# Two chained model blocks on one core: the norm in front of the expert queries made behind the projection ahead of it, search rounds of the key selection placed elsewhere, and filler products left out at three stages

## The chip, the cores and the metric

The kernel runs on one core of one Trainium2 chip. The metric is the device time of one launch in microseconds (us), as the median of several runs. Everything is float32, batch 1, 512 tokens, model width 1024.

## The reference, cut to what matters

The reference chains two model blocks. The first one mixes the tokens (a state space branch and a forgetting attention, merged, then projected by `w_out` and added to x) and then applies a product-key expert layer. The second has two layers, of which the even one has a sparse attention with an index search and a differential attention. The parts that the change touches:

```python
def rms_norm(x, g):                 # both blocks: x * rsqrt(mean(x*x) + eps) * g

def peer_ffn(h, w_query, sub_keys, u_tab, v_tab):       # h = rms_norm(x, ffn_norm_g)
    q = (h @ w_query).reshape(bsz, seq, 8, 2, 128)
    scores = jnp.einsum('blhcd,hckd->blhck', q, sub_keys)     # 16 x 128 scores a token
    s_top, i_top = lax.top_k(scores, 16)
    ...

def dsa_mixer(...):                 # sparse attention: scores of an indexer, best 128 keys of each query
    rel = jax.nn.relu(einsum('bqhd,bsd->bqhs', iq, ik) * IDX_DIM ** -0.5)
    score = jnp.einsum('bqhs,bqh->bqs', rel, iw)
    score = jnp.where(causal, score, -jnp.inf)
    _, idx = lax.top_k(score, k_sel)
    ...

def diff_mixer(...):                # two softmaxes a head, the second subtracted
    p = safe_softmax(s, causal)
    a = p[:, :, 0] - lam_full * p[:, :, 1]
    ...
```

## The kernel before, in words

**Stages.** The program is a row of stages. Each is a block with one instruction stream for each engine, and no engine enters the next stage before all have left the one before. x is kept transposed, as `xT`: 8 tiles of 128 channels by 512 tokens.

**Float32 products.** A float32 product is made as three products of halves (L137, L138, L139): the high half of each operand is made by ScalarE (`high_half`, L121), the low half by VectorE or GpSimd (`low_half`, L126). A tile of a projection is 128 output channels by 512 tokens, 8 tiles deep: 24 products. `projection` runs turns of `per_turn` tiles. SyncE loads the weights of a tile, ScalarE makes their high half as soon as the tile four earlier is through TensorE, GpSimd the low half, TensorE multiplies, and functions given as `evacuate` read the result; `before`, `after`, `between` and `behind_tile` add work of a stage at named places. `spin` (L132) issues products of a mask that nobody reads.

**The end of the first mixing.** `merge` (L2384) ends with the `w_out` projection (`project_add`): 8 tiles `ps` are added to `xT` by VectorE (L848) behind each tile.

**Expert queries (`peer_scores`, L2639).** The stage starts with `Norm`: ScalarE squares the 8 tiles of `xT` (L245), TensorE sums them with a matrix of ones (L250), then runs 30 spins, ScalarE takes the root (L257), VectorE inverts it (L269), then writes each normalised tile into `room` (L278); ScalarE and VectorE make its halves `h_high` and `h_low`, tile by tile. TensorE turns the sub keys in the wait (16 transposes, L2664, which need the keys' DMA, L2656) and then runs 16 query tiles in 4 turns of 4. ScalarE copies each query tile (L2691), TensorE multiplies it by its keys (L2679), ScalarE copies the scores (L2686), and VectorE searches the 16 best of them: MAX8 and its index, MATCH_REPLACE8, MAX8 and index again, each for 4 token tiles (L2767, L2770, L2774). Turns 1 to 3 are a hardware loop on VectorE, whose waits are made with register arithmetic (L71). A pair of copies (L2704) closes a turn. Behind the last tile TensorE makes products for the expert stage (`early_scores`).

**The even layer of block two.** `index_scores` makes the indexer's scores. The 128 best keys of a query are found in 16 rounds of `take_best` (MAX8, L3795, then MATCH_REPLACE8, L3798), for token tile [1] alone and for tiles [2, 3] together; tile 0 needs none. The rounds of tile [1] stand in `index_scores`, one behind each index head's step at t = 2 and at t = 3. Round 0 of [2, 3] stands in front of the differential attention's query tiles (`lead`), rounds 1 to 6 beside the query tiles, 7 and 8 inside the differential attention (`paired_attention`, L1483, by `beside` at its steps s = 1 and 2), 9 to 14 in front of `tile_norm`'s VectorE part in the following projection (`nope`), 15 behind it.

**Paired attention (L1483).** It is used three times (differential attention, sparse attention, odd layer). Each call starts with `spin(c, 0, 8)` on TensorE; then each step makes two sets of scores (L1551), VectorE takes the maxima (L1670), ScalarE the exponentials (L1614), GpSimd and VectorE scale and subtract them (L1633, L1663), TensorE transposes them and multiplies by the values (L1581).

The projection that ends the even layer's attention already does what `Feed` and `Late` say: in `project_add` with `next_gain` ScalarE makes the high half of gain * x (L321) and the squares (L323) behind each tile, VectorE the low half (L335) and the running sum (L339); the next stage sums that over channels (L363, L366), and its root follows late, beside products.

## Time and profile before

| | |
|---|---|
| median of 3 runs | 3316.16 us (3311.45 to 3322.05) |
| profiled execution | 3321.01 us, its span 3319.2 us |
| mean granted TensorE clock | 0.983 |
| TensorE busy | 97% of the span |
| VectorE, ScalarE, GpSimd busy | 54%, 41%, 39% |
| differential attention's stage | from about 2015 us to about 2065 us of the span |
| merge's last product to the first work of the stage behind the queries | 525.75 us to 667.67 us |

Each row of a timeline is start, duration, engine, line, operation, output and inputs, and how many instructions it groups; in brackets stands how long the engine was idle ahead of it and what released it. 97% is a mean over the whole span: at a stage's border or at a wait the engine stands still, and those places have to be read from the timeline.

### The profile page before, as it was taken

The numbers are of one execution on the slowest core, as the hardware profiler recorded it, in microseconds if no ns is written. First come the engines' busy times: TensorE is split into PE (matmuls) and PEld (weight loads), VectorE is DVE, ScalarE is ACT, GpSimd is POOL, SyncE is SP. The second block draws the span as 40 slices with busy tenths as digits, with TensorE's granted clock in tenths as the row PEclk, the third lists the DMA queues.
The fourth block names the chain that finished last, engine by engine and source line by source line (L and its number), as shares of the span: only waits on it lengthen the run. The fifth ranks groups of instructions, "written<-read, shape, count | busy, mean of one in ns | idle before, by whom it ended". The sixth has DMA issues, their size and how long they took to land. (4 is left out here: it accounts for less than half of the span.)

```text
span 3319.2 us, 47973 instructions
## 1 busy us (share of the span) xinstructions
PE 3208.2 (97%) x16487; PEld 2656.5 (80%) x16492; DVE 1779.2 (54%) x3737; ACT 1353.8 (41%) x2338; POOL 1286.2 (39%) x788
## 2 busy tenths in 40 slices
PE   7999999989999999999999998999999999999999
PEld 6877787889988888888888865578887874578887
DVE  6515324888958777777877467542211226632211
ACT  5234433247763333333333455332222436632322
POOL 2223352368852222222221323444444337644443
PEclk9999999999999999999999999999999989999999
DMA  5321242146679999999997421033333520033322
GB/s 126 84 73 33 76 114 78 57 138 212 224 286 344 321 325 321 328 317 330 318 323 263 118 54 36 13 95 95 95 91 93 130 64 1 18 91 95 100 85 82
DMA packets 453450, 501.83 MB, mean 151 GB/s; under 512 B 77360, under 2 KB 397808, under 8 KB 435392
## 3 DMA queue, kind: packets, MB, share of 16 engines
q1 hardware_dynamic: 429792, 363.05, 35.7%
q0 software_dynamic: 18432, 134.23, 11.0%
q10 hardware_dynamic: 5088, 2.75, 0.3%
q8 instruction: 82, 1.34, 0.2%
q14 instruction: 56, 0.46, 0.0%
HBM read 457.86 MB, written 38.80 MB: 150 GB/s over the span
## 5 line engine op out<-in xcount | busy, mean ns | idle before, releaser
L126 POOL TENSOR_TENSOR w_low<-w_ring,w_high 128x1024 fp32r<-128x1024 f32 (+2 forms) x316 | 745.2, 2362 | 1102.1 <-ACT w_high L121 1073.1
L137 PE MATMUL ps<-h_low,w_high 128*128 128x512 f32 (+1 forms) x2432 | 904.4, 372 | 27.3 <-PEq L640 15.4
L139 PE MATMUL ps<-h_high,w_low 128*128 128x512 f32 (+1 forms) x2432 | 896.7, 369 | 0.0
L138 PE MATMUL ps<-h_high,w_high 128*128 128x512 f32 (+1 forms) x2432 | 895.9, 368 | 0.0
L137 PEld LDWEIGHTS ps<-h_low,w_high 128*128 128x128 f32 x2432 | 460.1, 189 | 93.3 <-POOLq L629 14.1
L138 PEld LDWEIGHTS ps<-h_high,w_high 128*128 128x128 f32 x2432 | 460.4, 189 | 58.8 <-issue 1.0
L139 PEld LDWEIGHTS ps<-h_high,w_low 128*128 128x128 f32 x2432 | 459.6, 189 | 56.4
L121 ACT ACTIVATE w_high<-w_ring 128x1024 fp32r<-128x1024 f32 (+3 forms) x318 | 323.7, 1023 | 138.3 <-PE ps L139 121.2
L139 PE MATMUL ps<-v_high,top_at 128*128 128x512 f32 x768 | 300.3, 391 | 0.0
L138 PE MATMUL ps<-v_high,top 128*128 128x512 f32 x768 | 300.2, 391 | 0.0
L137 PE MATMUL ps<-v_low,top 128*128 128x512 f32 x768 | 299.0, 389 | 0.0
L121 ACT ACTIVATE v_high<-w_ring 128x1024 fp32r<-128x1024 f32 x128 | 135.5, 1059 | 261.4 <-PE ps L139 261.4
L2536 POOL DMA_INDIRECT room<-in_peer_uv_dram,idx_now x62 | 89.8, 1448 | 340.5 <-DVE sums L3391 340.5
L1633 POOL TENSOR_SCALAR probs<-probs,stat 128x128 f32<-128x128 f32 (+3 forms) x153 | 158.7, 1050 | 94.8 <-DVE stat L1644 57.1
L139 PEld LDWEIGHTS ps<-v_high,top_at 128*128 128x128 f32 x768 | 144.1, 188 | 30.2
L848 DVE TENSOR_TENSOR xT<-xT,ps 128x512 f32<-128x512 f32 (+1 forms) x40 | 27.5, 687 | 262.0 <-PE ps L139 262.0
L137 PEld LDWEIGHTS ps<-v_low,top 128*128 128x128 f32 x768 | 144.2, 188 | 28.5 <-issue 0.3
L138 PEld LDWEIGHTS ps<-v_high,top 128*128 128x128 f32 x768 | 144.1, 188 | 28.5
L126 DVE TENSOR_TENSOR v_low<-w_ring,v_high 128x1024 fp32r<-128x1024 f32 x128 | 156.1, 1219 | 0.0
L2536 POOL DMA_INDIRECT ring<-in_peer_uv_dram,idx_now x63 | 81.2, 1288 | 161.1 <-DVE sums L3391 132.4
L137 PE MATMUL ps<-a_low,w_high 128*128 128x512 f32 x352 | 136.9, 389 | 0.0
L138 PE MATMUL ps<-a_high,w_high 128*128 128x512 f32 x352 | 136.9, 389 | 0.0
(551 smaller groups left out, 5398.8 us busy)
## 6 DMA issues: line engine op xcount, KB each, us to landing
w_ring<-in_peer_uv_dram SPq DMA_DIRECT2D x128, 512.0 KB, 5.7
u_raw<-in_peer_uT_dram SPq DMA_DIRECT2D x78, 512.0 KB, 5.7
w_ring<-in_peer_uT_dram SPq DMA_DIRECT2D x50, 512.0 KB, 3.8
w_ring<-in_ffn_w_gate_dram SPq DMA_DIRECT2D x44, 512.0 KB, 3.7
w_ring<-in_ffn_w_up_dram SPq DMA_DIRECT2D x44, 512.0 KB, 3.8
w_ring<-in_w_in_dram SPq DMA_DIRECT2D x36, 512.0 KB, 3.8
w_ring<-in_ffn_w_down_dram SPq DMA_DIRECT2D x32, 448.0 KB, 3.7
peer_gates<-room SPq DMA_DIRECT2D x6, 2048.0 KB, 8.0
```

Source lines behind the costliest of these rows:

```text
L121: return nc.scalar.activation(rounded(high), whole, ACT.Copy)
L126: return eng.tensor_tensor(rounded(low), whole, high, ALU.subtract)
L137: nc.tensor.matmul(out, rounded(w_high), rounded(x_low), start=start, stop=False, **more)
L138: nc.tensor.matmul(out, rounded(w_high), rounded(x_high), start=False, stop=False, **more)
L139: return nc.tensor.matmul(out, rounded(w_low), rounded(x_high), start=False, stop=stop, **more)
L848: nc.vector.tensor_tensor(d, d, c.ps[:, first_bank + b + (tiles * (i % 2) if alternate else 0), :], ALU.add).then_inc(bank_free, w.parts)
L1633: nc.gpsimd.tensor_scalar(of, of, inverse[:, s % p_bufs, a:a + 1], None, ALU.mult).then_inc(normed_pool, 1)
L2536: self.c.nc.gpsimd.indirect_dma_start(self.ring[slot], None, self.uv, bass.IndirectOffsetOnAxis(ap=index, axis=0)).then_inc(self.gathered[ ...
```

## The change

1. **Norm in front of the expert queries.** `merge` is given the gain of the expert layer's norm and passes it to `project_add`, which so feeds the next stage as the even layer's does: L321, L323, L335, L339 run behind each of the 8 `w_out` tiles, and 16 spins end the stage on TensorE. `peer_scores` uses `Late` for the sum and the root. The first turn's 4 query tiles are made from gain * x without the norm's factor, and their scores are scaled for each token while ScalarE copies them (4 copies of 128x128 instead of one of 128x512). VectorE writes the normalised x into `room`; the new class `Renewed` rewrites `h_high` during the first turn's last tile (ScalarE, tile by tile, each behind the product that reads the old one), the odd low halves on VectorE, ahead of its second search, the even ones on GpSimd between two weight tiles. The key transposes stand behind the first query tile. VectorE's search is written out instead of looped.
2. **Search rounds.** Of tiles [2, 3], rounds 1 to 7 now stand beside the query tiles, none in the attention, 8 to 14 in front of `tile_norm`'s VectorE part, 15 behind it as before. Of tile [1], the 8 rounds of t = 2 stay, the other 8 stand at the end of the differential attention's VectorE program (`behind`).
3. **Spins.** The `spin(c, 0, 8)` at the start of the three paired attentions is left out.

```diff
@@ class Renewed (new)
+    def normalise(self, dve):
+        c = self.c
+        for k in range(KD):
+            c.nc.vector.scalar_tensor_tensor(self.whole[:, k, :], c.xT[:, k, :], c.gains[:, k:k + 1], c.rstd[:, :], ALU.mult, ALU.mult).then_inc(self.normed, 1)
+
+    def high_halves(self, act, wait_last):
+        for k in range(KD):
+            act.wait_ge(self.normed, k + 1)
+            if k < KD - 1:
+                act.wait_ge(self.used, k + 1)
+            else:
+                wait_last()
+            high_half(self.c.nc, self.c.h.high[:, k, :], self.whole[:, k, :]).then_inc(self.high, 1)
+
+    def low_halves(self, waiting, eng, odd):
+        c = self.c
+        for k in range(odd, KD, 2):
+            waiting.wait_ge(self.high, k + 1)
+            low_half(eng, c.h.low[:, k, :], self.whole[:, k, :], c.h.high[:, k, :]).then_inc(self.low[odd], 1)
+
+    def wait(self, pe, k):
+        pe.wait_ge(self.low[k % 2], k // 2 + 1)
@@ projection, gpsimd
         body(0, w.split)
-        turn_loop(pool, body, 1)
+        if renewed is not None:
+            body(1, 0, 2)
+            renewed.low_halves(pool, nc.gpsimd, 0)
+            body(1, 2)
+        turn_loop(pool, body, 1 if renewed is None else 2)
@@ projection, tensor
+                    if renewed is not None and b == 0 and not (isinstance(i, int) and i == 0):
+                        renewed.wait(pe, k)
...
+                    if renewed is not None and isinstance(i, int) and (i, b) == (0, per_turn - 1) and k < w.kt[b] - 1:
+                        mm.then_inc(renewed.used, 1)
@@ project_add
-            how["tail"] = (6, 16)
+            how["tail"] = (6 if alternate or first is None else 0, 16)
@@ paired_attention
-                spin(c, 0, 8)
...
+                if behind is not None:
+                    behind(dve)
@@ merge
-        project_add(c, w_out, c.xT, mixed_halves, ahead=ahead, first=first, ctx=ctx, ready=ready, first_bank=4)
+        project_add(c, w_out, c.xT, mixed_halves, ahead=ahead, next_gain=next_gain, first=first, ctx=ctx, ready=ready, first_bank=4)
@@ peer_scores
+        late, renewed = Late(c, ctx, rows=True), Renewed(c, ctx, room)
...
         def turn_keys(pe):
             pe.wait_ge(keys_in, 16)
+            pe.wait_ge(late.rooted, late.n)
...
-                nc.scalar.activation(scores[:, b, :, :], c.ps[:, 4 + b, :], ACT.Copy).then_inc(scores_out, 1)
+                if isinstance(i, int) and i == 0:
+                    for t in range(TT):
+                        last = nc.scalar.activation(scores[:, b, t, :], c.ps[:, 4 + b, t * P:(t + 1) * P], ACT.Copy, scale=c.rstd_rows[:, t:t + 1])
+                    last.then_inc(scores_out, 1)
+                else:
+                    nc.scalar.activation(scores[:, b, :, :], c.ps[:, 4 + b, :], ACT.Copy).then_inc(scores_out, 1)
 
             for b in range(per_turn):
+                if isinstance(i, int) and i == 0 and b == per_turn - 1:
+                    renewed.high_halves(act, lambda: wait_tile(b))
...
             for b in range(per_turn):
+                if i == 0 and b == 1:
+                    renewed.low_halves(dve, nc.vector, 1)
...
+        def prepare(dve):
+            late.invert(dve)
+            late.wait(dve)
+            renewed.normalise(dve)
...
-        project(c, w_query, {"act": copy, "pe": score, "dve": search}, ahead=ahead, after={"pe": early_scores}, before={"sp": load_keys, "pe": turn_keys, "act": move_keys}, norm=Norm(c, ctx, gain, c.h, squares=room))
+        project(c, w_query, {"act": copy, "pe": score, "dve": search}, ahead=ahead, after={"pe": early_scores},
+                before={"sp": load_keys, "pe": late.sum, "act_first": late.root, "act": move_keys, "dve": prepare},
+                between={1: {}}, behind_tile={(0, 0): turn_keys}, unrolled=("dve",), renewed=renewed)
@@ even layer
-                subln["dve"] = lambda dve: (search(dve, 0, 6), given(dve), search(dve, 6, None))
+                subln["dve"] = lambda dve: (search(dve, 0, 7), given(dve), search(dve, 7, None))
-    beside_tiles = 2 * DIFF_H - 2
+    beside_tiles = 2 * DIFF_H - 1
-    rest = [(n, tiles) for n in range(beside_tiles + 1, beside_tiles + 3)]
-
-    def beside(dve, s):
-        if 1 <= s <= len(rest):
-            take_best(c, Chain(dve, c.dve_step), score, best, left, rest[s - 1][1], rest[s - 1][0])
+
+    def behind(dve):
+        for n in range(DSA_H, rounds):
+            take_best(c, Chain(dve, c.dve_step), score, best, left, [1], n)
-    paired_attention(c, [head(s) for s in range(DIFF_H)], beside=beside, spare=oT[:, 0:2, :])
-    late = range(beside_tiles + 3, rounds)
+    paired_attention(c, [head(s) for s in range(DIFF_H)], spare=oT[:, 0:2, :], behind=behind)
+    late = range(beside_tiles + 1, rounds)
@@ index_scores
-            if t >= 2:
+            if t == 2:
                 take_best(c, step, score, best, left, [1], n - IH)
```

(The views of `weighed` in the expert stage are given names of their own at the same addresses.)

**TensorE from `merge` into the query stage.** Before, from merge's last product to the first query product (branch rows are the stage's border):

```order
L139 MATMUL ps<-mixed_high,w_low 128x512
L515 UNCONDITIONAL_BRANCH
L498 UNCONDITIONAL_BRANCH
L250 MATMUL ps<-room,ones 128x512 x8
L132 MATMUL ps<-mask_causal,mask_ident 128x512 x30
L2664 MATMUL ps<-ident,keys 128x128 x16
L579 UNCONDITIONAL_BRANCH
L579 ISA
L137 MATMUL ps<-h_low,w_high 128x512
```

The same place in the changed kernel, and below the gap the end of its first query tile:

```order
L139 MATMUL ps<-mixed_high,w_low 128x512
L132 MATMUL ps<-mask_causal,mask_ident 128x512 x16
L549 UNCONDITIONAL_BRANCH
L532 UNCONDITIONAL_BRANCH
L397 MATMUL ps<-ones,sum_squares 128x1 x4
L400 MATMUL ps<-sum_squares,ones 128x512
L137 MATMUL ps<-h_low,w_high 128x512
...
L139 MATMUL ps<-h_high,w_low 128x512
L2710 MATMUL ps<-ident,keys 128x128 x16
L137 MATMUL ps<-h_low,w_high 128x512
```

The 8 sums and 30 spins have left the front of the stage, 5 short sums stand there, 16 spins stand in the stage before, and the transposes come after the first query tile.

**VectorE in the search of the scores.** One tile of the loop before:

```order
L2767 MAX turn_top<-scores 128x8 x4
L71 REGISTER_ALU
L2770 MAX_INDEX turn_top_at<-turn_top,scores 128x8 x4
L71 REGISTER_ALU
L2774 MATCH_REPLACE scores<-turn_top,scores 128x128 x4
L71 REGISTER_ALU
L2767 MAX turn_top<-scores 128x8 x4
L71 REGISTER_ALU
L2770 MAX_INDEX turn_top_at<-turn_top,scores 128x8 x4
L71 REGISTER_ALU x2
```

The changed kernel from its preparation to the second tile's first search row:

```order
L414 RECIPROCAL rstd_rows<-rstd_rows 128x4
L416 RECIPROCAL rstd<-rstd 128x512
L303 SCALAR_TENSOR_TENSOR room<-xT,next_gains,rstd 128x512 x8
L2834 MAX turn_top<-scores 128x8 x4
L2837 MAX_INDEX turn_top_at<-turn_top,scores 128x8 x4
L2841 MATCH_REPLACE scores<-turn_top,scores 128x128 x4
L2834 MAX turn_top<-scores 128x8 x4
L2837 MAX_INDEX turn_top_at<-turn_top,scores 128x8 x4
L126 TENSOR_TENSOR h_low<-room,h_high 128x512 x4
L2834 MAX turn_top<-scores 128x8 x4
```

The register rows are gone in all 16 tiles, and 4 low halves stand between the first and the second search.

**VectorE in the differential attention.** Before, from the border into its first steps:

```order
L1635 UNCONDITIONAL_BRANCH
L1670 TENSOR_REDUCE stat<-ps 128x1 x4
L1644 RECIPROCAL stat<-stat 128x2
L1647 TENSOR_TENSOR stat<-stat,minus 128x1
L3795 MAX sum_squares<-left_343 128x8
L3795 MAX sum_squares<-left_344 128x8
L3798 MATCH_REPLACE left_343<-sum_squares,left_343 128x384
L3798 MATCH_REPLACE left_344<-sum_squares,left_344 128x512
L1670 TENSOR_REDUCE stat<-ps 128x1 x2
```

In the changed kernel the start, and below the gap its end (the pair of L3859 and L3862 stands there 8 times):

```order
L1676 UNCONDITIONAL_BRANCH
L1711 TENSOR_REDUCE stat<-ps 128x1 x4
L1685 RECIPROCAL stat<-stat 128x2
L1688 TENSOR_TENSOR stat<-stat,minus 128x1
L1711 TENSOR_REDUCE stat<-ps 128x1 x2
...
L1577 COPY probsT<-ps 128x2x128
L3859 MAX sum_squares<-score 128x8
L3862 MATCH_REPLACE score<-sum_squares,score 128x256
L3859 MAX sum_squares<-score 128x8
```

Nothing of the search stands between the maxima any more; 8 rounds of tile [1] stand behind the last copy of probabilities.

## Rows read from the trace of the kernel before

**Rows 1.** Busy time in stretches (us, then PE, PEld, DVE, ACT, POOL, clock)
```profile
554.00:650.00 96.00, 95.91 (x480) 80.92 (x478) 72.93 (x434) 30.99 (x46) 36.24 (x15) 1.00 0.25 71
```
**Rows 2.** Timeline, from merge's last product into the second query tile
```profile
525.75 0.39 PE L139 MATMUL ps<-mixed_high,w_low 128*128 128x512 f32 x1
529.07 0.87 SPq L2656 DMA_DIRECT2D keys<-in_peer_sub_keys_dram  x1
...
537.93 6.64 PE L132 MATMUL ps<-mask_causal,mask_ident 128*128 128x512 bf16 x30
...
544.41 1.91 PE L2664 MATMUL ps<-ident,keys 128*128 128x128 f32 x16
546.07 0.48 PE L137 MATMUL ps<-h_low,w_high 128*128 128x512 f32 x1
...
553.69 0.40 PE L137 MATMUL ps<-h_low,w_high 128*128 128x512 f32 x1
```
**Rows 3.** Timeline at two borders of the even layer: late norm sums' template
```profile
2198.75 0.39 PE L139 MATMUL ps<-o_high,w_low 128*128 128x512 f32 x1
...
2203.48 0.47 PE L137 MATMUL ps<-h_low,w_high 128*128 128x512 f32 x1 [0.88 <-PEq L640]
...
2573.40 1.10 PE L366 MATMUL ps<-sum_squares,ones 128*128 128x512 f32 x2
```
**Rows 4.** DMA issues, 520 to 560 us: median us to landing
```profile
keys<-in_peer_sub_keys_dram SPq DMA_DIRECT2D x1, 0.5 KB, 6.8
```
**Rows 5.** Timeline of VectorE (one row GpSimd), search of the query scores and the stage behind
```profile
561.60 0.87 DVE L2767 MAX8 turn_top<-scores 128x8 f32<-128x128 f32 x4 [8.76 <-ACT scores L2686]
...
612.45 2.54 POOL L126 TENSOR_TENSOR w_low<-w_ring,w_high 128x1024 fp32r<-128x1024 f32 x1 [2.95 <-ACT w_high L121]
612.65 2.49 DVE L2704 COPY top_at<-turn_top_at 128x256 uint32 x1
...
660.27 0.87 DVE L2767 MAX8 turn_top<-scores 128x8 f32<-128x128 f32 x4 [0.42 <-DVE turn_top_at L2770]
661.30 0.09 DVE L2770 MATCH_VALUE_LOAD turn_top_at<-turn_top,scores 128x8 f32 x1 [0.15 <-DVE turn_top L2767]
...
666.37 0.29 DVE L2704 COPY top<-turn_top 128x256 f32 x1 [0.34 <-DVE turn_top_at L2770]
...
668.69 0.99 DVE L2767 MAX8 best<-work 128x8 f32<-128x50 f32 x8
669.72 0.09 DVE L2770 MATCH_VALUE_LOAD best_at<-best,work 128x8 f32 x1
```
**Rows 6.** Timeline of TensorE, first work behind the query stage
```profile
667.82 0.55 PE L2996 MATMUL ps<-ident,h_high 128*128 128x128 f32 x1 [8.28 <-PEq L488]
```
**Rows 7.** Timeline, last rotation and start of the differential attention
```profile
2013.17 0.75 DVE L970 SCALAR_TENSOR_TENSOR qkT<-ps,of_turn,cos 128x512 f32<-128x512 f32 x1 [3.23 <-ACT ps L948]
...
2015.84 1.89 PE L132 MATMUL ps<-mask_causal,mask_ident 128*128 128x512 bf16 x8 [1.57 <-PEq L515]
...
2020.14 1.15 DVE L3795 MAX8 sum_squares<-left 128x8 f32<-128x384 f32 x2
...
2023.23 0.58 ACT L1614 ACTIVATE probs<-ps,stat 128x384 f32<-128x384 f32 x1 [2.55 <-DVE stat L1670]
```
**Rows 8.** Timeline, end of the differential attention on VectorE
```profile
2057.54 0.42 DVE L1535 COPY probsT<-ps 128x256 f32<-128x256 f32 x1
...
2065.22 1.15 DVE L3795 MAX8 sum_squares<-left 128x8 f32<-128x384 f32 x2 [7.25 <-PEq L1538]
```
**Rows 9.** Timeline of VectorE in the index stage, rounds of tile [1]
```profile
1948.16 0.42 DVE L3795 MAX8 sum_squares<-score 128x8 f32<-128x256 f32 x1
...
1949.13 0.62 DVE L3775 SCALAR_TENSOR_TENSOR score<-room,weights,score 128x384 f32<-128x384 f32 x1
```
**Rows 10.** Busy time in two stretches of the differential attention
```profile
2026.00:2034.00 8.00, 4.92 (x19) 2.53 (x21) 7.40 (x22) 3.59 (x13) 3.68 (x3) 0.50 0.00 1
2034.00:2055.00 21.00, 16.96 (x97) 8.81 (x95) 18.02 (x55) 14.39 (x48) 11.48 (x10) 0.97 0.00 1
```

36 lines of the change are left out of this document (22 added, 14 removed).

## The prediction

> **What bounds the kernel now.** I read the page first, then busy time by stretches, then the timeline around each place that the diff names. The reader is to see in [rows 1] that through the query tiles TensorE is busy 95.91 of 96 us at the full clock: work taken from another engine there gains nothing unless TensorE can start the tiles sooner or leave the stage sooner. So the places that can pay are its holes. There are three kinds. The first is the front of the query stage [rows 2]: the last useful product of `merge` starts at 525.75, the first query product at 546.07, 20.32 us later, and the tile it opens lasts until 553.69, 7.62 us where 24 products need 5.45 (0.227 start to start, the pitch at which TensorE runs every full tile here). The second is the end of that stage [rows 5, 6]: TensorE has stood still for 8.28 us when the next stage gives it work, since VectorE's search ends last, at about 666.9. The third lies in the differential attention [rows 7, 8], where ScalarE waits 2.55 us for maxima that stand behind a search round.
>
> **Part 1, the front of the query stage.** Removed from TensorE's path: 8 sums, 30 spins (6.64 us), the root, the inversion, the first normalised tile. The nearest template is a border of the same form in the even layer [rows 3]: last product at 2198.75, 16 spins, first product of the next stage at 2203.48, 4.73 us. To it come 5 sums; the wide one of them takes 0.55 (1.10 for two, [rows 3]), the 4 short ones less than that together, so about 1.0 in all. First product: 525.75 + 4.73 + 1.0 = 531.5, its tile ends at 536.9 if nothing feeds it slowly. Behind it stand the transposes, which want the keys. SyncE issues those 3.3 us after the last product now (529.07); with the spins in front of the border it enters the stage when TensorE does in the template, so at 530.4, and 6.8 us to landing [rows 4] gives 537.2. With 1.91 us for the transposes the second tile starts at 539.1 instead of 553.69: **14.5 us sooner**. Of this about 0.5 goes back at the end of the first turn: ScalarE must write the last high half before it copies the fourth query tile, and TensorE waits for that copy. Net 14.0. In `merge` ScalarE and VectorE get 0.6 to 0.75 us each of squares, halves and sums behind a tile of 5.45; TensorE's tiles cover that, and without the cover it would cost about 2 us a tile. The 4 scaled copies of scores take up to 1.2 us instead of 0.6; nothing but the search waits for them.
>
> **Part 1, the end.** Three chains end there. (a) TensorE's: 667.82 - 8.28 = 659.5 before, less 14.0 is 645.5. (b) The scores' copies are sooner by the same 14.0, and the last search can end at about 644. (c) VectorE's order. Its first search starts about 14 us sooner than 561.60 [rows 5], at 547.5, but the second stands behind the odd low halves, whose last one waits for the end of the fourth tile: 539.1 + 3 x 5.45 + 2 x 0.8 (scores) = 557.1, plus about 0.95 for the last high half and 0.75 for the low one, 558.8. Then 15 searches. One takes 6.19 us in the loop: 5.77 from 660.27 to the end of the last index (666.37 less its 0.34 of idle) and 0.42 of idle before. Inside it stand four register gaps of 0.15; where the same three operations are written out, the gap is 0.03 (668.69 + 0.99 against 669.72). So the written-out search is 5.77 - 4 x 0.12 + 0.1 = 5.4. 15 x 5.4 = 81, plus three closing pairs of copies inside (0.5 each, or 2.7 where one falls beside GpSimd, 612.65) and one at the end, about 4.5: 644.3. The longest is (a), 645.5, with the usual 0.8 us of border 646.3 instead of 667.67: 21.3 sooner. Three chains within 1.5 us of each other seldom all run as planned, so I take **20**. If the gaps stay (the loop's pace of 6.19), (c) ends 15 x 0.79 = 12 us later, at 656, and the gain is 11; that is the lower bound, 21.3 the upper one.
>
> The copy of 2.49 us in rows 5 began 0.2 us after a GpSimd low half of 2.54 and ended with it; its like takes 0.29 elsewhere. In the changed stage 4 even low halves on GpSimd, an estimated 1.2 us each (half of a 128x1024 one), run beside 4 odd ones on VectorE. If each odd one had to wait for its neighbour, only the last would show, up to 1.2 us on chain (c): 645.5, still level with (a). The Trainium skill (SBUF — State Buffer, Terms) says that VectorE and GpSimd share a port pair that is lock-allocated, "the loser fully blocks". The row agrees with it; by it the sum would keep 20, without it 21.3 would be open.
>
> **Part 2, the search rounds.** The round that VectorE makes at 2020.14 [rows 7] is about 2.5 us and the wait behind it 2.55; there are two such rounds, both in the attention's ramp, where nothing covers them: -5.0. The seventh round goes beside the last query tiles, where VectorE stands idle for 3.23 us ahead of its last rotation [rows 7]: 0. The 8 rounds of tile [1] leave the index stage. Its timeline shows TensorE at the next projection's tiles before VectorE is through with the last index step, so I take 0; it can't be a loss. They cost 0.97 us each [rows 9] behind the attention, 7.8 together; VectorE has 7.25 us of idle there [rows 8], between its last copy (ends 2057.96) and the next stage, so the border comes 0.8 later (0.3 of barrier counted). The seventh round in front of `tile_norm`'s part makes that later by 2.5; how much of it TensorE waits for lies between 0 and 2.5, and I take the middle, 1.3. Part 2: -5.0 + 0.8 + 1.3 = **-2.9**. Bounds: 0 (if the maxima wait for TensorE instead) and -5.
>
> **Part 3, the spins.** Each block of 8 takes 1.82 us start to start [rows 7]; it stands three times between a border and the first scores. Two give 1.8 each; at the differential attention a table load that ran beside the spins may show 0.3. Together **-5.1**. Less only if another engine is later than TensorE; bounds 0 and -5.5. More could come: [rows 10] show TensorE at 0.50 (1.2 GHz) from 2026 to 2034, after the waits that part 2 removes. If it kept 2.4 GHz there, its 4.92 us of work would halve at best: -2.5, not in my sum.
>
> **A rule against part 3.** In the rows TensorE falls to 0.50 behind waits, spins in front of them or not. The Trainium skill (TensorE: Matmul & The Clock Gate, Part 1) says that "the default state is throttled, and activity releases the throttle". By that rule, leaving out activity at three starts is a risk and not a gain; what it would make of the time is the last rival below.
>
> **Sum.** -20 - 2.9 - 5.1 = -28.0 against the profiled execution's 3321.0, that is 3293.0. The profiled one lies 4.9 above the median of the runs, 3316.16, so the median should come to **3288**. What a measurement of this kernel can tell from no change is about 0.3%, 10 us: the change must gain more than that to count as faster.
>
> **Rivals.**
> *The search keeps its pace.* If the 0.15 gaps are the chip's and not the registers', VectorE ends last and part 1 gives 11: 3316.2 - 19 = 3297. For it: the loop's gaps stand also where no loop turns. Against: 0.03 in written-out code, rows 5. Chance 0.12.
> *The freed time is eaten inside.* TensorE waits at the fifth tile for low halves (GpSimd makes them between two weight tiles, in order, so a late high half holds both the weights and x), or the keys land late. Each tile of delay is 5.45; with two of them and no gain in part 2 the total is 28 - 11 - 3 - 4 = 10 or less: 3306 to 3316. For it: three engines in a chain within one tile. Against: each link is 0.6 to 1.2 us and has 5.45. Chance 0.08.
> *The change does not do what it says*: products now start before the keys and the norm are there, and another wait (the gains' load, the border) simply takes the spins' place, so that the front stays at 15 us or more. The template of rows 3 speaks against it. Time 3308 or so; chance 0.03.
> *The clock falls.* With no spins, each paired attention runs its first 21 us at 1.2 GHz. TensorE was busy 16.96 of 21 us there at 0.97 [rows 10]; at half the clock it would need 33.9, 13 more in each of three, 39 in all: 3316.2 - 28 + 39 = 3327, **slower**. It decides once more than 38 us are lost, so all three must stay low for the whole 21 us. For it: 0.50 did occur in this ramp. Against: it occurred with the spins, and the clock was back by itself. Chance 0.03. Partly (one attention, 13 us) it only narrows the gain to 3301; chance 0.04, within the range.
>
> **How the numbers follow.** The forecast has 0.70, its own range 3283 to 3295. The range is 3279 to 3303: down to 3279 for the unspent 1.3 and 2.5 and the runs' own spread of 5 us, up to 3303 for the pace rival and one slow attention. Faster is 0.70 + 0.12 + 0.04 = 0.86, same 0.08 + 0.03 = 0.11, slower 0.03.
>
> **What would show it.** Right: the first query product about 6 us after `merge`'s last; transposes ending near 539; register gaps gone and a search pitch of 5.4 in the rows; the work behind the query stage near 646; no ScalarE wait of 2.5 us at the attention's second and third step; scores directly at its border. Wrong: a TensorE wait for `h_low` at the fifth tile, a search pitch of 6.2, DVE work at the border later than ScalarE's and TensorE's by more than 1 us behind the differential attention, or granted clocks of 0.50 over whole attentions.

## The result and the profile after

| | before | changed |
|---|---|---|
| median of 16 runs each | 3320.89 us (3311.45 to 3332.47) | 3302.59 us (3295.25 to 3311.16) |
| profiled execution, span | 3321.01, 3319.2 us | 3309.44, 3307.3 us |
| mean granted TensorE clock, profiled | 0.983 | 0.981 |
| TensorE idle ahead of the work behind the query stage | 8.28 us | 13.82 us |

The ratio is 0.9950, 95% interval 0.9940 to 0.9959: faster by 0.5%, 16.6 us, where 28 were forecast. (The medians differ by 18.3 us, the two profiled executions by 11.6.) The runs of one kernel differ with the mean clock that they were granted: over all runs of this study, those of one kernel lie 2.26 us lower for each 0.001 of clock. Comparisons of kernels below go by ratio and interval; where they are close, the mean "at clock 0.984" is given too, which is each run moved by that slope (3316.1 before with 55 runs, 3302.6 changed; by this measure the change is worth 13.5 us).

The stretches of the profiled executions, from starts of TensorE's rows (my differences; the last column is changed minus before):

```
                                                             before  changed
merge's last product to first query product                   20.32     7.07   -13.25
first query product to first work behind the query stage     121.75   129.35    +7.60
differential attention, first scores to last values           43.54    38.05    -5.49
last values to the next stage's first product                  4.50     7.28    +2.78
that product to the sparse attention's first scores           34.73    34.47    -0.26
```

The front gained 13.25 us and the rest of the stage gave 7.60 back: the query stage is 5.65 us shorter and not 20. The attention gained 5.49 and its border gave 2.78 back. The last row is shorter by 0.26 only although 8 spins (1.8 us) have left it.

The front of the query stage in the timeline of the changed kernel, the rows that answer to [rows 2]:

```profile
527.21 0.39 PE L139 MATMUL ps<-mixed_high,w_low 128*128 128x512 f32 x1
527.44 3.63 PE L132 MATMUL ps<-mask_causal,mask_ident 128*128 128x512 bf16 x16
...
532.57 0.87 SPq L2699 DMA_DIRECT2D keys<-in_peer_sub_keys_dram  x1
...
532.85 1.02 PE L397 MATMUL ps<-ones,sum_squares 128*128 128x1 f32 x8 [1.78 <-PEq L191]
533.74 1.10 PE L400 MATMUL ps<-sum_squares,ones 128*128 128x512 f32 x2
534.28 0.95 PE L137 MATMUL ps<-h_low,w_high 128*128 128x512 f32 x1
...
535.03 0.63 PE L138 MATMUL ps<-h_high,w_high 128*128 128x512 f32 x1
...
541.74 1.91 PE L2710 MATMUL ps<-ident,keys 128*128 128x128 f32 x16
...
543.41 0.47 PE L137 MATMUL ps<-h_low,w_high 128*128 128x512 f32 x1
```

To be seen: the border takes 5.64 us from the last product to the first sum (4.73 in the template); the sums take 1.43 us and not 1.0, of which the wide one has the 0.54 that was forecast (533.74 to 534.28) and the four short ones 0.89 (532.85 to 533.74; each float32 matmul leaves two rows, so that 4 show as 8); and the first 8 or so of the first tile's 24 products take 0.63 us each instead of 0.39. The tile takes 7.46 us. The clock of that stretch and those of the attention's start, by windows (us of the window, us busy of PE, PEld, DVE, ACT, POOL, then the granted clock):

```profile
534.00:542.00 8.00, 8.00 (x29) 6.08 (x29) 6.21 (x7) 1.79 (x3) 2.38 (x1) 0.79 1.01 289
2010.90:2014.90 4.00, 3.41 (x18) 1.49 (x18) 1.48 (x6) 3.04 (x9) 0.61 (x1) 0.73 0.01 4
2014.90:2018.90 4.00, 3.73 (x15) 1.47 (x13) 3.10 (x10) 2.12 (x7) 1.23 (x2) 0.50 0.00 0
```

VectorE's rows in the query stage, with one of ScalarE and one of GpSimd, that answer to [rows 5, 6]:

```profile
551.90 0.88 DVE L2834 MAX8 turn_top<-scores 128x8 f32<-128x128 f32 x4 [7.30 <-ACT scores L2735]
...
557.97 4.61 ACT L121 ACTIVATE h_high<-room 128x512 fp32r<-128x512 f32 x8
...
559.18 6.01 DVE L126 TENSOR_TENSOR h_low<-room,h_high 128x512 fp32r<-128x512 f32 x4 [1.52 <-ACT h_high L121]
...
559.51 6.83 POOL L126 TENSOR_TENSOR h_low<-room,h_high 128x512 fp32r<-128x512 f32 x4
...
565.12 0.86 DVE L2834 MAX8 turn_top<-scores 128x8 f32<-128x128 f32 x4
...
571.21 0.87 DVE L2834 MAX8 turn_top<-scores 128x8 f32<-128x128 f32 x4 [0.35 <-DVE turn_top_at L2837]
...
583.52 2.48 DVE L2760 COPY top_at<-turn_top_at 128x256 uint32<-128x256 uint32 x1
...
662.54 0.29 DVE L2760 COPY top_at<-turn_top_at 128x256 uint32<-128x256 uint32 x1
...
663.63 0.77 PE L3063 MATMUL ps<-ident,h_high 128*128 128x128 f32 x2 [13.82 <-PEq L522]
```

To be seen: the four odd low halves take 6.01 us (0.69 each elsewhere) while GpSimd's four even ones take 6.83; the second search starts at 565.12; the next ones follow every 6.1 us with 0.35 of idle in front, not every 5.4; VectorE ends at 662.83, and TensorE has been idle for 13.82 us when it is given work again. So VectorE sets the end of the stage more than before. (In the kernel before, the loop's pitch was 6.2 us: without the register rows a search is only 0.1 us shorter.)

The differential attention of the changed kernel, the rows that answer to [rows 7, 8]:

```profile
2010.93 0.49 PE L1593 MATMUL ps<-qkT 64*128 64x128 f32 x4 [1.64 <-PEq L549]
...
2015.55 0.58 ACT L1655 ACTIVATE probs<-ps,stat 128x384 f32<-128x384 f32 x1 [1.60 <-DVE stat L1711]
...
2047.12 0.42 DVE L1577 COPY probsT<-ps 128x256 f32<-128x256 f32 x1
...
2047.45 0.42 DVE L3859 MAX8 sum_squares<-score 128x8 f32<-128x256 f32 x1
...
2055.81 1.15 DVE L3859 MAX8 sum_squares<-left 128x8 f32<-128x384 f32 x2 [0.53 <-PEq L1580]
2056.26 0.47 PE L137 MATMUL ps<-h_low,w_high 128*128 128x512 f32 x1 [3.56 <-PEq L678]
```

The wait of ScalarE for maxima is 1.60 where it was 2.55, the search rounds are gone from it. But the 8 rounds of tile [1] start at 2047.45, VectorE is only 0.53 us ahead of the border, and TensorE waits 3.56 us for the next stage, as against 0.78 before.

### The profile page after: what moved, and what is told of

It is laid out like the page before. It is cut to its first block and busy times, and to the rows that moved or that the text cites. A ratio compares the mean times of both kernels' runs of the same rounds, so it can differ in the third digit from the quotient of the medians.

```text
span 3307.3 us, 47824 instructions
## 1 busy us (share of the span) xinstructions
PE 3194.6 (97%) x16443; PEld 2653.4 (80%) x16448; DVE 1792.0 (54%) x3751; ACT 1359.9 (41%) x2359; POOL 1293.2 (39%) x792
## 5 line engine op out<-in xcount | busy, mean ns | idle before, releaser
L139 PE MATMUL ps<-v_high,weighed_low 128*128 128x512 f32 x768 | 300.7, 392 | 0.0
L138 PE MATMUL ps<-v_high,weighed_high 128*128 128x512 f32 x768 | 300.5, 391 | 0.0
L137 PE MATMUL ps<-v_low,weighed_high 128*128 128x512 f32 x768 | 299.6, 390 | 0.2 <-DVE v_low L126 0.2
L139 PEld LDWEIGHTS ps<-v_high,weighed_low 128*128 128x128 f32 x768 | 144.2, 188 | 30.1
L137 PEld LDWEIGHTS ps<-v_low,weighed_high 128*128 128x128 f32 x768 | 144.4, 188 | 29.4 <-DVE v_low L126 0.9
L138 PEld LDWEIGHTS ps<-v_high,weighed_high 128*128 128x128 f32 x768 | 144.2, 188 | 28.3
```

The lines of the kernel that those rows point to most:

```text
L137: nc.tensor.matmul(out, rounded(w_high), rounded(x_low), start=start, stop=False, **more)
L138: nc.tensor.matmul(out, rounded(w_high), rounded(x_high), start=False, stop=False, **more)
L139: return nc.tensor.matmul(out, rounded(w_low), rounded(x_high), start=False, stop=stop, **more)
```

## The experiments

The same stretches in the profiles of all kernels that ran (front: merge's last product to first query product; query: from there to the first work behind the stage; attention and border as above; nope: first product to the sparse attention's first scores):

```
kernel                        front   query  attention  border   nope   ratio to before
before                        20.32  121.75    43.54     4.50   34.73
changed                        7.07  129.35    38.05     7.28   34.47   0.9950
e1_norm_alone                  7.07  129.38    43.50     4.47   34.74   0.9970
e2_no_ticks                    7.07  117.16    36.56     7.17   34.50   0.9911
e3_low_on_gpsimd               7.07  123.46    37.73     7.00   34.47   0.9927
e4_both                        7.07  117.92    37.74     7.29   34.52   0.9926
e5_spins_back                  7.07  127.74    36.31     7.18   36.31   0.9978
e6_rounds_as_before            7.06  129.35    41.08     4.46   34.54   0.9960
e7_no_ticks_rounds_in_index    7.07  118.77    40.88     4.47   35.90   0.9936
e8_no_ticks_sums_behind        5.79  119.99    37.80     6.93   34.52   0.9922
e9_before_no_ticks            20.33  116.72    43.04     4.47   34.75   0.9980
e10_rounds_split               7.07  117.17    37.90     4.46   31.87   0.9900
```

These stretches have a spread of their own, part of which comes from the granted clock. The first tile of the query stage is an example. In the changed kernel, e1, e3, e6 and e7 the second query tile starts 16.2 us behind merge's last product; in e2, e4, e5 and e10, whose instructions up to there are the same, it starts 14.6 us behind it, because the first tile ran at the full clock. In e5 that window reads

```profile
531.44:539.44 8.00, 8.00 (x44) 6.71 (x43) 6.49 (x7) 3.29 (x7) 2.40 (x1) 1.00 1.07 302
```

against 0.79 above. So 1.6 us of any difference in the query stage can be this. Kernels are best compared in pairs with the same first tile: the changed kernel with e1, e3, e6 and e7, and e5 with e2, e4 and e10.

**e1_norm_alone: part 1 without parts 2 and 3.** The edit undoes both: `spin(c, 0, 8)`, `beside`, `rest` and `t >= 2` stand as in the kernel before.

```diff
+                spin(c, 0, 8)
                 for s in range(n_steps + lag):
...
-            if t == 2:
+            if t >= 2:
                 take_best(c, step, score, best, left, [1], n - IH)
```

> The changed kernel with only the norm moved in front of the expert queries: the search rounds and the spins of the even and odd layers stand as before. Theory (the query stage is ended by VectorE's search, which starts late and keeps its pace): the work behind the query stage starts about 5.7 us sooner against merge's last product than before, TensorE is idle some 14 us ahead of it (8.3 before), ratio to the kernel before 0.9980 to 0.9985. Rival (the stage gains the 10 to 14 us that its front gains, and the rest of the change loses them): ratio 0.9958 to 0.9970.

Measured: 3310.15 us, ratio 0.9970 (0.9957 to 0.9984), a little more than expected (3308.6 at clock 0.984, so -7.5). The ratio is at the edge of the rival's 0.9958 to 0.9970, but the rows decide: the front and the query stretch are the changed kernel's to 0.03 us. The theory holds: part 1 is worth 5.6 us in its stage.

```profile
663.77 0.77 PE L3064 MATMUL ps<-ident,h_high 128*128 128x128 f32 x2 [13.83 <-PEq L522]
```

TensorE again stands still for 13.8 us there: what the front gained is spent in front of this row.

**e2_no_ticks: the search without the extra semaphore increments.** In the loop a wait is written by `hold`, which issues the wait and then increments a semaphore of its own (the tick). The change wrote the loop out, but its calls kept `hold`.

```diff
-            step = Chain(dve, c.dve_step, i, per_turn * 5 * TT + 2, c.dve_tick)
+            step = Chain(dve, c.dve_step, i, per_turn * 5 * TT + 2)
...
-                hold(dve, scores_out, i * per_turn + (b + 1), c.dve_tick)
+                dve.wait_ge(scores_out, i * per_turn + (b + 1))
```

> The changed kernel, with VectorE's waits in the query search written as plain waits, without the extra semaphore increment (the tick) behind each. Theory (the 0.14 and 0.35 us gaps of the search are the ticks' cost): the gaps fall to about 0.03 and 0.1, the pitch of a search from 6.1 to 5.4, the search ends 8 to 10 us sooner, the work behind the stage starts 8 to 10 us sooner, total 3302.6 - 9 = 3293 or so (ratio about 0.9922). Rival (the gaps are how long VectorE takes to see its own results with this shape): pitch 6.1 as in the changed kernel, ratio 0.9950, no change.

Measured: 3287.87 us, ratio 0.9911 (0.9892 to 0.9931). The search's rows and the next stage's first work:

```profile
562.72 0.87 DVE L2834 MAX8 turn_top<-scores 128x8 f32<-128x128 f32 x4
...
564.92 0.88 DVE L2834 MAX8 turn_top<-scores 128x8 f32<-128x128 f32 x4
...
568.18 0.87 DVE L2834 MAX8 turn_top<-scores 128x8 f32<-128x128 f32 x4
...
570.38 0.87 DVE L2834 MAX8 turn_top<-scores 128x8 f32<-128x128 f32 x4
```
```profile
635.29 0.88 DVE L2834 MAX8 turn_top<-scores 128x8 f32<-128x128 f32 x4 [0.49 <-ACT scores L2738]
...
643.83 0.34 PE L139 MATMUL ps<-h_high,w_low 128*128 128x384 f32 x1
...
646.42 0.29 DVE L2760 COPY top_at<-turn_top_at 128x256 uint32<-128x256 uint32 x1
...
647.41 0.67 PE L3063 MATMUL ps<-ident,h_high 128*128 128x128 f32 x2 [3.25 <-PEq L522]
```

The pitch is 5.46 us (564.92 to 570.38), no idle is left at a tile's border where the scores are there, and TensorE waits 3.25 us instead of 13.82. VectorE is still last, 2.5 us behind TensorE's last product, but it has caught up: its last search but one, at 635.29, had to wait for the scores. From merge's last product to the next stage's work it is 124.23 us, 12.2 fewer than in the changed kernel. Of these 1.6 are the clock of the first tile: against e5, whose first tile is like this one's, it is 10.6 fewer (134.81 to 124.23), and e7 against the changed kernel gives 10.6 too (136.42 to 125.84). The median fell by 14.7; at clock 0.984 by 7.4, because part of the median's fall is a higher granted clock (0.9865 in the mean of its runs, 0.9838 in the changed kernel's), which one can't put down to this edit with 6 runs. The rows are clear, the theory holds: the gaps were ticks.

**e3_low_on_gpsimd: all low halves of the renewed x on GpSimd.**

```diff
-        for k in range(odd, KD, 2):
+        for k in range(KD):
...
-                if i == 0 and b == 1:
-                    renewed.low_halves(dve, nc.vector, 1)
```

> The changed kernel, with all 8 low halves of the normalised x made by GpSimd instead of the odd ones by VectorE. Theory (VectorE's and GpSimd's low halves hold each other up, 6.0 us for 4 and 6.8 us for 4, and the second search waits for them): GpSimd takes about 1.2 us each alone, 9.6 in all from about 559.5 to 569; VectorE's second search starts at about 558 instead of 565; the search ends about 6 to 7 us sooner; TensorE may wait 1 us or less in the fifth tile; ratio about 0.9932. Rival (TensorE and the weights behind the halves on GpSimd lose what VectorE gains): TensorE waits 3 us or more in the fifth to seventh tile and the ratio is 0.9945 or above.

Measured: 3295.92 us, ratio 0.9927 (0.9906 to 0.9949). The groups of the low halves of x between 520 and 700 us, first of the changed kernel (busy us, mean ns):

```profile
L126 POOL TENSOR_TENSOR h_low<-room,h_high 128x512 fp32r<-128x512 f32 x4 | 6.8, 1737 | 0.0
L126 DVE TENSOR_TENSOR h_low<-room,h_high 128x512 fp32r<-128x512 f32 x4 | 5.9, 1512 | 1.6 <-ACT h_high L121 1.5
```

and of this one, with TensorE's only wait for them and its first work behind the stage:

```profile
L126 POOL TENSOR_TENSOR h_low<-room,h_high 128x512 fp32r<-128x512 f32 x8 | 10.0, 1300 | 0.0
```
```profile
574.18 0.50 PE L137 MATMUL ps<-h_low,w_high 128*128 128x512 f32 x1 [0.28 <-POOL h_low L126]
...
662.31 0.77 PE L3061 MATMUL ps<-ident,h_high 128*128 128x128 f32 x2 [7.18 <-PEq L522]
```

Alone GpSimd needs 1.30 us each and not the 1.2 of my estimate; together with VectorE it needed 1.74 and VectorE 1.51 instead of 0.69. The eight took 7.2 us side by side (559.18 to 566.34), where alone they add to 8.0, so side by side saves hardly anything. The stage is 5.9 us shorter, and TensorE waits 0.28 us for the last half. The theory holds with 5.9 for the 6 to 7. At clock 0.984 it is worth 2.3 us only, which is less than the rows show; why stays open.

**e4_both: e2 and e3 together.** The edit is both diffs above.

> The changed kernel with both edits: no ticks in the search and all low halves on GpSimd. Theory: VectorE is no longer last; the stage is ended by TensorE's products, which ended at 649.8 in the changed kernel, or by the last search behind the last scores; the work behind the stage starts at about 651 instead of 663.5, 12 us sooner: total about 3291, ratio 0.991. Rival (the two savings overlap and VectorE remains last for another reason): no more than the better of the two alone, ratio 0.9922 or above.

Measured: 3295.74 us, ratio 0.9926 (0.9908 to 0.9945).

```profile
658.87 0.77 PE L3061 MATMUL ps<-ident,h_high 128*128 128x128 f32 x2 [3.25 <-PEq L522]
```

The ratio is the rival's: no more than the better edit alone. Its reason is not, since the stage ends 11.4 us sooner than in the changed kernel, about the 12 that the theory set as the floor; e2 alone reaches that. TensorE's idle ahead of the next stage is 3.25 us as in e2_no_ticks, and the two stretches add to 124.99 against 124.23. Once the ticks are gone VectorE catches up with the scores, so TensorE sets its pace, and a VectorE that starts its second search sooner gains nothing.

**e5_spins_back: the changed kernel with the three blocks of spins.** `spin(c, 0, 8)` back in `paired_attention`.

```diff
+                spin(c, 0, 8)
```

> The changed kernel with the 8 spins back at the start of the three paired attentions. Theory (the spins only stood in the way): the first scores come 1.8 us later behind the border in each of the three, everything else as in the changed kernel, so 5 us slower than the changed kernel: 3307.5, ratio 0.9965. Rival (without spins TensorE works through the differential attention's ramp at 1.2 GHz, 0.57 to 0.63 from 2012 to 2025 in the changed kernel, and that costs what the spins cost): granted clock 0.9 or more in the attention's first 8 us behind the first scores, the attention itself 1 to 3 us shorter from first scores to last values than the 38.05 of the changed kernel, ratio 0.9950 or less.

Measured: 3309.64 us, ratio 0.9978 (0.9966 to 0.9990), so 7 us slower than the changed kernel by medians, 6.8 at clock 0.984, and 9 by ratio, with an interval of about 5 around it. At the differential attention the clock differs (windows of 4 us from the first scores on; the last column but two is the clock; the first pair is of e5, the second of e2, which has no spins):

```profile
2003.70:2007.70 4.00, 3.62 (x23) 1.54 (x22) 2.44 (x9) 2.20 (x9) 0.61 (x1) 1.00 0.00 0
2007.70:2011.70 4.00, 2.32 (x15) 1.14 (x13) 3.90 (x14) 3.02 (x12) 2.54 (x3) 0.87 0.00 0
```
```profile
1988.57:1992.57 4.00, 3.44 (x22) 1.54 (x22) 2.24 (x8) 3.18 (x10) 0.61 (x1) 1.00 0.01 4
1992.57:1996.57 4.00, 2.42 (x17) 1.09 (x16) 3.43 (x14) 3.32 (x12) 2.92 (x3) 0.90 0.00 0
```

With the spins the first 4 us run at 1.00 (0.73 in the changed kernel), the next at 0.87 (0.50), and the attention is 36.31 us instead of 38.05, which gives back 1.74 of the 1.8 that they take. But e2 ran at 1.00 and 0.90 without any spins and took 36.56. The first 4 us ran at 1.00 in all four profiles with spins (before, e1, e5, e9) and in one of eight without them, where the other seven had 0.66 to 0.76. So the spins make the full clock likelier there, and what they give back lies between 0.25 and 1.74 us: whether they are neutral is not settled. At the sparse attention the nope stretch is 1.84 us longer with them. The rest of the 7 must lie at the third one and in the spread, since the long stretch up to the odd layer's first scores differs by 3.4 us between the two profiles (540.81 against 537.39), and by as much among kernels that are alike there. So the spins do cost, at least in the two places that start at the full clock without them.

**e6_rounds_as_before: part 2 undone.**

```diff
-                subln["dve"] = lambda dve: (search(dve, 0, 7), given(dve), search(dve, 7, None))
+                subln["dve"] = lambda dve: (search(dve, 0, 6), given(dve), search(dve, 6, None))
...
-            if t == 2:
+            if t >= 2:
```

> The changed kernel with the search rounds placed as before (part 2 undone). Theory (the two rounds cost the attention 5.5 us, and the 8 rounds behind it give 2.8 of that back at the border, while the next stage ends level): the differential attention lasts 43.5 us from first scores to last values instead of 38.05, from there to the next stage's first product 4.5 instead of 7.28, so about 2.7 us slower than the changed kernel: 3305.3, ratio 0.9957. Rival (part 2 gives back all it gains by the sparse attention's first scores): 3302.6, ratio 0.9950.

Measured: 3303.63 us, ratio 0.9960 (0.9948 to 0.9972); at clock 0.984 3302.0 against 3302.6. These runs do not tell the theory from the rival: by ratio it is 3 us slower than the changed kernel, with an interval of about 5 around it, at clock 0.984 it is 0.6 faster. The rows favour the rival. The two rounds cost the attention 3.0 us without spins (41.08 against 38.05), and what is saved goes at the border (4.46 against 7.28): attention, border and nope stretch together are 0.3 us apart. With spins the two rounds cost 7.2 (43.50 in e1 against 36.31 in e5) and the three stretches are 2.9 apart, but the totals of e1 and e5 show no gain (0.9970 and 0.9978). Part 2 is worth nothing that these runs can tell.

**e7_no_ticks_rounds_in_index: e2 with the rounds of tile [1] back at t = 3 of the index stage.**

```diff
-            if t == 2:
+            if t >= 2:
...
-    paired_attention(c, [head(s) for s in range(DIFF_H)], spare=oT[:, 0:2, :], behind=behind)
+    paired_attention(c, [head(s) for s in range(DIFF_H)], spare=oT[:, 0:2, :])
```

> The kernel without ticks in the query search, and with the 8 rounds of tile [1] back in the index stage at t = 3 instead of behind the differential attention; the rounds of tiles [2, 3] stay as in the changed kernel. Theory (in the index stage they are hidden by TensorE, behind the attention they hold the border): from last values to the next stage's first product 4.5 us instead of 7.2, no lower granted clock at that stage's start, the index stage to the attention's first scores unchanged, 3 to 4 us faster than the same kernel without this edit (3287.9): 3284.5, ratio 0.990. Rival (the index stage pays them): the stretch up to the first scores grows by 3 us or more and the total stays 0.9911.

Measured: 3296.66 us, ratio 0.9936 (0.9916 to 0.9956), against 0.9911 of e2; at clock 0.984 it is 3294.2 against 3295.2. Inconclusive as a total. The border, from the last values to the next stage's first product, is 4.47 us instead of 7.17, as expected. But the profiled attention ran at 0.50 to 0.66 for its first 16 us and took 40.88 (in e10, whose attention is the same program, it took 37.90), and in the projection behind it TensorE waits:

```profile
2038.77 2.42 PE L1623 MATMUL ps<-probsT,vb 128*128 128x512 f32 x8 [1.12 <-ACT probsT L1661]
...
2043.24 0.47 PE L137 MATMUL ps<-h_low,w_high 128*128 128x512 f32 x1 [0.75 <-PEq L678]
...
2060.82 1.01 PE L3501 MATMUL ps<-ident,roots 128*128 128x128 f32 x3 [2.81 <-DVE roots L3509]
```

The seventh round in front of `tile_norm`'s part holds the roots by 2.81 us. TensorE comes to this row 17.58 us behind the stage's first product here and 17.78 in the changed kernel, where it has no wait: there its own products, at a lower clock behind the late border (0.64 over the first 4 us), took the time that is a wait here. The rival's place, the index stage, shows nothing: from its first score sum on VectorE to the attention's first scores it is 75.36 us here and 75.16 in the changed kernel.

**e8_no_ticks_sums_behind: e2 with the norm's sums behind the first query tile.**

```diff
         def turn_keys(pe):
+            late.sum(pe)
             pe.wait_ge(keys_in, 16)
-            pe.wait_ge(late.rooted, late.n)
             for n in range(quarters):
+                if n == 2:
+                    pe.wait_ge(late.rooted, late.n)
```

> The kernel without ticks in the query search, and with the norm's sums issued behind the first query tile, not in front of it. Theory (the sums' 1.4 us stand on TensorE's path to the first product, and the 1.0 us of 128x1 sums behind 1.8 of idle lets the clock fall to 1.2 GHz for half of the first tile, 2.0 us): from merge's last product to the first query product 5.6 us instead of 7.07, the first tile 5.5 instead of 7.5, but then the keys (6.8 us from issue) come about 1 us after it; to the second tile 2 us are left of the gain; total about 3286, ratio 0.9905. Rival (the clock falls in any case at the border, the sums only move): first tile 7.4 again and the second tile no sooner, ratio 0.9911.

Measured: 3290.72 us, ratio 0.9922 (0.9906 to 0.9938): no gain. The front is 5.79 us, as the theory said, and the first tile takes 5.53 at full clock:

```profile
537.93 0.39 PE L139 MATMUL ps<-mixed_high,w_low 128*128 128x512 f32 x1
...
543.72 0.47 PE L137 MATMUL ps<-h_low,w_high 128*128 128x512 f32 x1 [1.93 <-PEq L678]
...
549.25 0.94 PE L397 MATMUL ps<-ones,sum_squares 128*128 128x1 f32 x8
...
552.94 0.48 PE L137 MATMUL ps<-h_low,w_high 128*128 128x512 f32 x1
```

But the full clock is not shown to come from moving the sums, since e2, e4, e5 and e10 have it with the sums in front. The second tile starts 15.0 us behind merge's last product, sooner than the changed kernel's 16.2 and later than the 14.6 of e2, which this kernel is to be compared with. So the second tile comes no sooner, as the rival says, though not for its reason. And the root comes later, and VectorE with it:

```profile
555.53 9.71 DVE L303 SCALAR_TENSOR_TENSOR room<-xT,next_gains,rstd 128x512 f32<-128x512 f32 x8
...
570.61 7.71 DVE L126 TENSOR_TENSOR h_low<-room,h_high 128x512 fp32r<-128x512 f32 x4
```

Writing the normalised x takes 9.71 us (5.39 in the changed kernel), beside GpSimd's weight halves, the odd low halves 7.71, and the whole stage ends 1.5 us later than in e2.

**e9_before_no_ticks: the kernel before with a written-out search without ticks.**

```diff
-            step = Chain(dve, c.dve_step, i, per_turn * 5 * TT + 2, c.dve_tick)
+            step = Chain(dve, c.dve_step, i, per_turn * 5 * TT + 2)
...
-                hold(dve, scores_out, i * per_turn + (b + 1), c.dve_tick)
+                dve.wait_ge(scores_out, i * per_turn + (b + 1))
...
+        project(c, w_query, ..., norm=Norm(c, ctx, gain, c.h, squares=room), unrolled=("dve",))
```

> The kernel before, and nothing of the change but a search of the query scores that is written out and has no ticks (and the renamed views that this needs). Theory (the ticks made VectorE last in that stage in both kernels; without them TensorE is last): search pitch 5.45 plus waits for scores, TensorE idle about 3.3 us ahead of the next stage's work instead of 8.3, that work 5 us sooner against merge's last product (137.1 us instead of 142.1), total 5 us faster than before, ratio 0.9985. With the norm moved as well it was 124.2 us, so 12.9 of the 17.8 us would be the norm's, once it isn't hidden by the search. Rival (written-out code alone carries most of the gain of 17.8): 130 us or less, ratio 0.9965 or less.

Measured: 3310.34 us, ratio 0.9980 (0.9967 to 0.9992).

```profile
667.21 0.77 PE L3000 MATMUL ps<-ident,h_high 128*128 128x128 f32 x2 [3.27 <-PEq L488]
```

20.33 + 116.72 is 137.05 us, as expected, 5.0 fewer than before, and TensorE waits 3.27. The theory holds. With it the norm's move is priced in both settings: 5.6 us (142.07 to 136.42) while the ticks stand, 12.8 us (137.05 to 124.23) once they are gone. With the first tile of the other clock it is 7.3 (to e5's 134.81) and 11.2 (to e7's 125.84). At either clock the norm's move is worth 5.6 us more without the ticks.

**e10_rounds_split: e7 with six rounds in front of `tile_norm`'s part and two behind.**

```diff
-                subln["dve"] = lambda dve: (search(dve, 0, 7), given(dve), search(dve, 7, None))
+                subln["dve"] = lambda dve: (search(dve, 0, 6), given(dve), search(dve, 6, None))
```

> The kernel without ticks, the rounds of tile [1] in the index stage, none in the differential attention, and of tiles [2, 3] six rounds (as in the kernel before) in front of tile_norm's VectorE part and two behind it. Theory (the seventh round in front of it made TensorE wait 2.81 us for the roots in the kernel with the rounds in the index stage): that wait is gone, from the projection's first product to the sparse attention's first scores 32.9 us instead of 35.90 (34.73 before, which has 8 spins more), about 2.5 us faster than that kernel; both parts together about 3286 on a median of clocks, ratio 0.9905. Rival (the eighth round behind holds the end of the projection): 35 us or more and no gain.

Measured: 3284.82 us (3280.26 to 3291.46), ratio 0.9900 (0.9882 to 0.9918); 3291.1 at clock 0.984, against 3294.2 of e7 and 3295.2 of e2. The wait for the roots is 0.28 us instead of 2.81. The nope stretch is 31.87 us (32.9 expected), 4.0 shorter than in e7; 2.5 are the wait, and 1.5 are the 32 products behind it, which took 5.36 us in e7 at a lower clock and 3.84 here:

```profile
2046.81 1.38 PE L3501 MATMUL ps<-ident,roots 128*128 128x128 f32 x10 [0.28 <-DVE roots L3509]
```

It is the fastest kernel of the study, 33 us below the kernel before and about 16 below the changed one by ratio (11.5 at clock 0.984).

## Why the prediction was right in sign and wrong in its largest term

**The front (forecast: second tile 14.5 us sooner, measured 11.7).** Mechanism right, two sizes off: the border with sums 7.07 us instead of 5.7 (0.9 of it border, 0.4 the four short sums), the first tile 7.46 instead of 5.45, at 0.79 of the clock over the stretch. The latter is in part the luck of the execution: with the full clock, as in e5, it would have been 13.3. The keys did not matter then: they were there in time for a tile that ended late. In e8, where the tile ended 11.3 us behind merge's last product, the sums and the transposes still followed it without a wait.

**"Three chains end there" (forecast 20, measured 5.65).** This is the step that failed, in its chain (c). I priced the search at 5.4 us by writing the loop out; measured were 6.1. I put the 0.15 us gaps down to register arithmetic, whose rows the order of instructions shows leaving, and took the 0.03 us of other written-out code for what would be left. That code has no ticks, and the changed search still had them; the semaphore instruction is not a row of either view. The register rows, which did leave, were worth 0.1 us a search (6.2 to 6.1). The rival "the search keeps its pace" was the case, with chance 0.12, though not for its reason (that the gaps are the chip's): e2 removed them. 15 searches and their copies took 97.7 us from 565.12, 85.5 forecast; 10.5 of the 12.2 are the pitch. The rival gave 3297 against a median of 3316.16; the measured ratio of 0.995 makes 3299.6 of it. That the two are near is in part luck: part 1 gave 5.65 us and not the rival's 11, part 2 nothing, and the spins and the spread the rest.

The other 4.9 us of chain (c) are 2.8 of the front and 2.1 of the odd low halves. There I had written that of four halves that wait for their neighbours on GpSimd only the last would show. But the high halves were made in 4.61 us and all four low ones had to queue: 1.51 us each where it is 0.69 alone. The Trainium skill (SBUF — State Buffer, Terms), "the loser fully blocks", agrees with these rows in the main: the eight operations took 7.2 us, where 8.0 is the sum of their times alone. Its rule was in my text, the count was wrong.

**Chain (a), TensorE's (forecast 14.0 sooner, measured 11.2).** From the two idle times: its last product came 133.8 us behind merge's in the kernel before and 122.6 in the changed one. It did not end the stage; without the ticks it paces VectorE, whose last search then ends 2.5 us behind it (e2). Chain (b) had put the end of that search 1.5 us ahead of it.

**Part 2 (forecast -2.9, measured none that the runs can tell: e6).** Parts 2 and 3 together made the attention 5.5 shorter in the profile, where 5.0 were forecast for the rounds alone; against e6 the rounds are 3.0 of it. The border cost 2.8 and not 0.8. The cover of 7.25 us that I subtracted was that of an attention whose last values ran at a lower clock (4.11 and 2.42 us for the last two groups of 8 products, 2.42 and 2.42 now): from VectorE's last copy, 2047.54, to the end of TensorE's last filler products, 2052.70, it is 5.2 us now (7.0 before), and the rounds take 7.8. In that border's shadow the clock fell again (0.64 from 2056 to 2060). The 1.3 us for the seventh round in front of `tile_norm`'s part did not show as a wait in the changed kernel, where TensorE was slower itself; in e7 it is 2.81 us.

**Part 3 (forecast -5.1, measured -7 by medians, -9 by ratio with an interval of about 5 around it: e5).** Right in size where TensorE stays at 2.4 GHz; at the differential attention the spins gave back between 0.25 and 1.74 of their 1.8 us. The last rival, a clock that stays at 1.2 GHz for 21 us, did not happen: it was low for about 10 us there in the changed kernel, 14 in e7, and at 1.00 at the two other starts. The Trainium skill (TensorE: Matmul & The Clock Gate, Part 1), activity releases the throttle, agrees with e5's 1.00 and 0.87 against 0.73 and 0.50, though e2 had 1.00 and 0.90 without the fillers; its price was 1.7 us at most, at one of three places.

## What to carry to other kernels

When an engine's pace is set by short instructions, look for what stands between them in the program text (waits, increments, register work), not only in the rows: the profile shows it as a gap of 0.1 us that no row explains, and such gaps were worth 10.6 us in this stage. Before a head start is counted, follow every engine to the end of the stage: of 13 us gained at the front 5.65 reached the end, and TensorE's idle there grew from 8.3 to 13.8. And a cover measured before the change (7.25 us of idle) shrinks with what the change itself removes. Last, compare like with like: one profile of each kernel puts 1.6 us of clock spread into the very stage that is being priced.

## What was not expected of the hardware

A semaphore increment issued by VectorE between a wait and the next instruction cost 0.11 us each time: with it 0.14 to 0.15 us passed from one group's end to the next, without it 0.03 (e2). The mean granted clock differs between runs of the same kernel (0.978 to 0.990 over the study) and explains most of their spread, 2.26 us for 0.001; with 6 runs the medians of two kernels can differ by 7 us for that reason alone, and stretches of the profile were the better measure. The clock at one and the same border differs between executions too. At the first query tile of the changed front, 1.78 us of idle and 1.0 us of 128x1 sums behind the border, it was 0.79 over 8 us in five profiles (changed, e1, e3, e6, e7) and 1.00 in four (e2, e4, e5, e10), with the same instructions up to there. What decides it these runs do not show; that the sums let it fall, as e8 supposed, is not shown either.
